# Low halves of plain weight blocks by a ScalarE negative and an accumulating DMA, in a two-layer backbone kernel

## The reference

```python
for l in range(2):
    mc, ml = modulation(c_ctx, w_mod, b_mod), modulation(c, w_mod, b_mod)   # 6 vectors each
    hc, hl = modulate(xc, mc[0], mc[1]), modulate(xl, ml[0], ml[1])
    # layer 0: attention and SSD mixer: u = h @ w_in ... out = [o_a, y] @ w_out
    # layer 1: pooling mixer: u = h @ w_in; pooled @ pool_w (4 groups) * pool_scale; @ w_out
    xc = layer_norm(ALPHA * xc + mc[2] * dc, ln1_g, ln1_b)                   # latent alike
    fc = square(relu(modulate(xc, mc[3], mc[4]) @ w_up)) @ w_down            # 1024 -> 4096 -> 1024
    xc = layer_norm(ALPHA * xc + mc[5] * fc, ln2_g, ln2_b)
```

## Time and profile before

| | us |
|---|---|
| median of 3 runs | 1476.22 (1473.55 to 1477.52) |
| the profiled execution's own time | 1473.62 |
| its span | 1471.8 |
| TensorE, VectorE, ScalarE, GpSimd busy | 1405.8, 1039.6, 542.7, 79.1 |
| mean granted TensorE clock | 0.989 |

### The profile page before, as it was taken

How to read it: one execution, slowest core, us unless ns; L and a number is a source line. 1 busy time by engine, 2 the same in 40 slices (tenths; PEclk the granted TensorE clock), 3 DMA queues, 4 the chain that set the end, 5 groups by cost and what they waited for, 6 DMA issues and landing times.

```text
span 1471.8 us, 22812 instructions
## 1 busy us (share of the span) xinstructions
PE 1405.8 (96%) x8806; PEld 1245.6 (85%) x8806; DVE 1039.6 (71%) x1645; ACT 542.7 (37%) x976; POOL 79.1 (5%) x146
## 2 busy tenths in 40 slices
PE   4999999899999999999999999989999999999996
PEld 3899988666788998998899879868999899889985
DVE  3694566677468976776776796757797677667678
ACT  3333353267435432332233244434443233223322
POOL 1300000011200000000000010001000000000001
PEclk8999999999999999999999999999999999999998
DMA  9701233596713322322221523542332232123141
GB/s 317 220 29 59 87 117 129 167 342 209 249 57 114 130 84 61 115 79 65 85 92 58 208 77 129 186 148 76 121 125 84 62 111 85 59 85 98 59 172 72
DMA packets 132300, 177.47 MB, mean 121 GB/s; under 512 B 4170, under 2 KB 104258, under 8 KB 131698
## 3 DMA queue, kind: packets, MB, share of 16 engines
q1 hardware_dynamic: 123250, 146.46, 31.0%
q0 software_dynamic: 7376, 26.76, 5.3%
q10 hardware_dynamic: 1584, 3.01, 0.5%
HBM read 166.94 MB, written 9.27 MB: 120 GB/s over the span
## 4 chain that ended last, share of the span: by engine, by line
PE 80%; DVE 8%; ACT 5%; DMA 3%; issue 2%; ACTq 0%; POOL 0%; SPq 0%; DVEq 0%
PE ps L779 40%; PE ps L1288 20%; PE ps L761 7%; PE ps L770 4%; PE ps L810 2%; DVE convT L1992 2%; PE ps L1105 2%; ACT h_full L1688 1%; DVE wlo L1896 1%; DMA gate_parts<-modrow 1%; ACT whi L1398 1%; ACT tmp L1688 1%; PE ps L1116 1%; ACT e_att L1608 1%; DMA raw<-in_w_mod_l 1%
## 5 line engine op out<-in xcount | busy, mean ns | idle before, releaser
L1398 ACT ACTIVATE whi<-raw 128x512 fp32r<-128x512 f32 (+2 forms) x186 | 175.4, 953 | 357.1 <-PE ps L779 294.0
L779 PE MATMUL ps<-whi,hid_hi 128*128 128x512 f32 x640 | 249.6, 390 | 0.0
L779 PE MATMUL ps<-wlo,hid_hi 128*128 128x512 f32 x640 | 249.2, 389 | 0.0
L779 PE MATMUL ps<-whi,hid_lo 128*128 128x512 f32 x640 | 249.1, 389 | 0.0
L1896 DVE TENSOR_TENSOR wlo<-raw,whi 128x512 fp32r<-128x512 f32 (+2 forms) x186 | 201.7, 1093 | 24.4 <-ACT whi L1398 21.0
L779 PE MATMUL ps<-whi,h_hi 128*128 128x256 f32 (+1 forms) x480 | 158.7, 331 | 8.7 <-DVE h_lo L2696 5.4
L2325 DVE TENSOR_TENSOR acc<-acc,ps 128x512 f32<-128x512 f32 x120 | 80.3, 684 | 122.0 <-PE ps L779 122.0
L779 PE MATMUL ps<-whi,h_lo 128*128 128x256 f32 (+1 forms) x480 | 153.9, 321 | 0.0
L779 PE MATMUL ps<-wlo,h_hi 128*128 128x256 f32 (+1 forms) x480 | 153.7, 320 | 0.0
L779 PEld LDWEIGHTS ps<-whi,hid_hi 128*128 128x128 f32 x640 | 120.1, 188 | 25.3 <-DVE wlo L1896 0.8
L779 PEld LDWEIGHTS ps<-whi,hid_lo 128*128 128x128 f32 x640 | 120.1, 188 | 25.2
(11 more groups left out here) (337 smaller groups left out, 2669.9 us busy)
## 6 DMA issues: line engine op xcount, KB each, us to landing
raw<-in_w_up_l SPq DMA_DIRECT2D x32, 1024.0 KB, 5.6
raw<-in_w_down_l SPq DMA_DIRECT2D x32, 1024.0 KB, 5.1
raw<-in_w_mod_l SPq DMA_DIRECT2D x28, 1024.0 KB, 5.5
raw<-in_w_in_l SPq DMA_DIRECT2D x12, 1024.0 KB, 5.3
raw_split<-in_w_mod_l SPq DMA_DIRECT2D x8, 1024.0 KB, 6.9
raw<-in_w_out_l SPq DMA_DIRECT2D x5, 1024.0 KB, 6.2
x_spill<-x_tok POOLq DMA_DIRECT2D x10, 512.0 KB, 2.9
x_tok<-x_spill POOLq DMA_DIRECT2D x10, 512.0 KB, 6.0
```

Source lines behind the costliest of these rows:

```text
L779: mm = pe.matmul(out, a_of(still, k), w_of(part, k), start=(first and k == 0 and part == 0 and still == 0), stop=(last and k == nk - 1 and ...
L1398: act.activation(ring_piece(whi, w, g), piece(w, g), ACT.Copy).then_inc(hi_done, 1)
```

## The change

For 26 blocks the low half is made another way. ScalarE, behind each piece of the high half, writes the negative of the raw piece, rounded to fp32r, into `wlo`. Then GpSimd issues a DMA that reads the same 1 MB of weights from HBM again and adds it to `wlo`. TensorE waits for that DMA's semaphore. The blocks are: w_out 1 to 3 of layer 0 and 0 to 3 of layer 1; up 2 and 3 and down 0, 1 and 12 to 15 of both layers; w_in 2 and 3 and the pool block of layer 1. The Strassen blocks, the down blocks between (two of them per turn in the loops and around them), and the two blocks that open each stage behind a norm stay with VectorE. The row stores of layer 1's modulation are issued by GpSimd. Several semaphores are merged. The source of a block's DMA is moved from SP's `load` to `block_source`, unchanged.

```diff
+        NORM_W = tuple(first + n for first in (W_UP[0], W_IN1, W_UP[1]) for n in range(2))
+        def added(w):
+            return w > W_OUT[0] and not strassen(w) and not (S[w_k[w]][0] == "down" and 2 <= S[w_k[w]][2] < 12) and w not in NORM_W
+        def low_ready(eng, w, i=None):
+            if added(w):
+                eng.wait_ge(low_in[w % 2], 16 * ADDED_IN[w])
+            else:
+                eng.wait_ge(lo_done, lin(OPS_LO[w + 1], PER_LO, i))
...
-                    sp.wait_ge(lo_done, lin(OPS[w_ord[j] + 1], PER, i))
+                    if added(w_ord[j]):
+                        sp.wait_ge(neg_done, ADDED[w_ord[j]])
+                    else:
+                        sp.wait_ge(lo_done, lin(OPS_LO[w_ord[j] + 1], PER_LO, i))
...
+            def add_low(w, i=None):                                     # GpSimd
+                pool.wait_ge(neg_done, ADDED[w])
+                src = block_source(w_k[w], i)
+                pool.dma_start(wlo[:, w % 2, :].rearrange("p (k n) -> p k n", n=src.shape[2]), src, accum_op=ALU.add) \
+                    .then_inc(low_in[w % 2], 16)
...
+            def store_rows(m):
+                pool.wait_ge(mod_row, m + 1)
+                for c in range(2):
+                    pool.dma_start(stored_at(m)[:, c], modrow[c:128:32, m % 2, :]).then_inc(tail_st[m % 2], 16)
...
             load_gate_rows(1, 3)
             fetch_x(LAT)
+            for j in range(1, 4):
+                if added(W_OUT[0] + j):
+                    add_low(W_OUT[0] + j)
...
             def mlp(layer):
-                spill_x(layer)
-                fetch_x_again(layer)
+                if added(W_UP[layer] + 2):
+                    add_low(W_UP[layer] + 2)
+                for t in range(LAT):
+                    spill_x(layer, t)
+                for kind, n, i in mlp_steps(pool):
+                    w = w_ord[S.index((kind, layer, n))]
+                    if added(w + 1):
+                        add_low(w + 1, i)
+                    if (kind, n) == ("up", 2):
+                        spill_x(layer, LAT)
+                    if (kind, n) == ("down", 12):
+                        fetch_x_again(layer)
+                if added(w_ord[S.index(("down", layer, 15))]):
+                    add_low(w_ord[S.index(("down", layer, 15))])
...
             norm_share(1)
+            add_low(W_IN1 + 2)
             for g in range(2, 4):
                 pool.wait_ge(pl_f, 2 * (g - 1))
                 pool.dma_start(ic[:, g % 2, :], A["t_icnt"][g].partition_broadcast(P)).then_inc(ic_ld[g % 2], 16)
-            pool.wait_ge(mod_tr, GATE_SUM[1])
-            load_gate_rows(2, 0)
-            pool.wait_ge(gate_rows_ld, 16 * 3)
+                add_low(W_IN1 + g + 1)
+            for m in range(M_TAIL, 48):
+                if m == 46:
+                    pool.wait_ge(mod_tr, GATE_SUM[1])
+                    load_gate_rows(2, 0)
+                    add_low(W_OUT[1])
+                store_rows(m)
+            add_low(W_OUT[1] + 1)
+            pool.wait_ge(sum_rows_ld, 16 * 6)
             load_gate_rows(3, 1)
             spread_gate(2)
+            add_low(W_OUT[1] + 2)
+            add_low(W_OUT[1] + 3)
...
                     act.activation(ring_piece(whi, w, g), piece(w, g), ACT.Copy).then_inc(hi_done, 1)
+                    if added(w):
+                        ins = act.activation(ring_piece(wlo, w, g), piece(w, g), ACT.Copy, scale=-1.0)
+                        if g == len(ring(w)) - 1:
+                            ins.then_inc(neg_done, 1)
...
-                tail_store(KT + f)                                      # ScalarE, in layer 1's pool stage
...
             def split_lo(w, i=None, ops=None):
+                if added(w):
+                    return
```

More of the change, by code:

```diff
@@ L462, in build, with block_source @@
         PER = 4 * len(PIECES) + 4 * 2
+        PER_LO = PER
+        NORM_W = tuple(first + n for first in (W_UP[0], W_IN1, W_UP[1]) for n in range(2))
+        def added(w):
+            return w > W_OUT[0] and not strassen(w) and not (S[w_k[w]][0] == "down" and 2 <= S[w_k[w]][2] < 12) and w not in NORM_W
+        OPS_LO = [0]
+        for w in range(nw):
+            OPS_LO.append(OPS_LO[-1] + (0 if added(w) else len(ring(w))))
+        ADDED = [sum(added(v) for v in range(w + 1)) for w in range(nw)]
+        ADDED_IN = [sum(added(v) and v % 2 == w % 2 for v in range(w + 1)) for w in range(nw)]
+        def low_ready(eng, w, i=None):
[3 more added lines that the diff above has]
+                eng.wait_ge(lo_done, lin(OPS_LO[w + 1], PER_LO, i))
+        def block_source(k, i=None):
+            kind, layer, n = S[k]
+            if kind == "up":
+                c0 = n * BW if i is None else bass.ds(i * (4 * BW) + n * BW, BW)
+                src = A[f"w_up_l{layer}"][:, slice(c0, c0 + BW) if i is None else c0]
+            elif kind == "down":
+                r0 = (n // 2) * CHUNK
+                rows = slice(r0, r0 + CHUNK) if i is None else bass.ds(i * (2 * CHUNK) + r0, CHUNK)
+                src = A[f"w_down_l{layer}"][rows, (n % 2) * 512:(n % 2) * 512 + 512]
+            elif kind == "out":
+                src = A[f"w_out_l{layer}"][(n % 2) * 512:(n % 2) * 512 + 512, (n // 2) * 512:(n // 2) * 512 + 512]
+            elif kind == "pool":
+                src = A["pool_w_l1"].rearrange("g k n -> (g k) n")
+            elif kind == "mod":
+                src = A[f"w_mod_l{layer}"][:, n * BW:(n + 1) * BW]
+            else:
+                src = A[f"w_{kind}_l{layer}"][:, n:n + BW]
+            return src.rearrange("(k p) n -> p k n", p=P)
         def at_ring(buf, its, cols=None):
@@ L690, in norm_share @@
                 for t in range(NT):
+                    if t == 3 and i < 3:
+                        for w in range(2):
+                            first = (W_UP[0], W_IN1, W_UP[1])[i] + w
+                            if added(first):
+                                add_low(first)
                     if i == 3 and t < LAT:
@@ L706, in norm_share, with spill_x @@
                     pool.tensor_tensor(lnrs[:, t, 1:2], lnve[:, t, 0:1], lnrs[:, t, 0:1], ALU.mult).then_inc(ln_rs, 1)
[L708 to L712, removed]
+            def spill_x(layer, t):
+                pool.wait_ge(ln_x, 2 * NT * layer + t + 1)
+                pool.dma_start(A["x_spill"][t * P:(t + 1) * P, :], x[:, t, :]).then_inc(x_re, 16)
             def fetch_x_again(layer):
@@ L1370, in _ @@
             w = W_IN1 + 4
-            pe.wait_ge(lo_done, OPS[w + 1])
+            low_ready(pe, w)
             for f in range(KT):
```

98 lines of the change are left out of this document (42 added, 56 removed).

## The result

| | before | after |
|---|---|---|
| median, us | 1474.88 (1473.52 to 1477.52, 4 runs) | 1609.84 (1606.78 to 1613.77, 4 runs) |
| ratio, 95% interval | 1 | 1.091 [1.088, 1.095] |
| span of the profiled execution | 1471.8 | 1609.3 |
| mean granted TensorE clock | 0.989 | 0.953 |

A forecast was written before the change was run, and what follows sets the result against it. TensorE, busy 96% of the span, was taken as the bound. 1473.6 + 76.8 of pauses + 23.2 of half clock + 2.6 to the median gave 1576 us, range 1520 to 1640; the forecast itself, 1537 to 1615, had chance 0.62.

The forecast's parts named there:

- The sum of the pauses: TensorE's added waits for late low halves at the listed blocks, thirteen terms: 76.8 us.
- T: Time from the end of ScalarE's negative to TensorE's release by the accumulating DMA: taken as 9.1 us.
- The prediction's three parts: Plain 1 MB GpSimd DMA 5.5 us, second read for the add 2.7, collision with SP's next weight load 0.9.
- 13T - 41.5: Thirteen pauses at the listed blocks, each the DMA's delay less that block's slack, added up: 76.8 us.
- the old 5.4 and 1.4: TensorE waits already there before the change: 5.4 us ahead of layer 1's w_out 0, 1.4 (u_pad) at w_in 2.
- The slack formulas: Per block, time from the negative's end to TensorE's first matmul on it; the pause is T less that.
- covered: Blocks with a preceding block's matmuls as cover, such as w_down 13 and 14 or the pool block: no pause.
- The half clock: TensorE at 1.2 instead of 2.4 GHz behind eight new pauses over 5.4 us, 2.9 each: 23.2 us.
- Stores, stream, merged waits: Layer 1's row stores on GpSimd, SP's weight load waiting for the negative, merged semaphores: each taken as 0.
- Relief of VectorE: VectorE's lighter queue: at most 0.8 of the 2.6 us before layer 1's first w_in block, taken as 0.
- The free add: Rival at the accumulating DMAs: they land like a plain transfer, 5.5 us, giving 1512 us; chance 0.17.
- The crawl: Rival at the accumulating DMAs: 13.6 us from negative to release, giving 1645 us; chance 0.17.

The follow-up runs named there:

- Serial: Changed kernel, but SyncE's next weight load into a raw buffer waits for the accumulating DMA instead of the negative: 1570.9 us, ratio 1.066.
- one_block: Kernel before, with only layer 1's last w_down block (15) made by negative and accumulating DMA: 1485.1 us, ratio 1.008.
- experiments 7 and 8: Kernel before with only layer 1's w_down 15 changed, without and with 30 idle matmuls during TensorE's wait: 1485.1 and 1483.2 us.
- experiments 9 and 10: Changed kernel with no block added, only row stores on GpSimd and merged semaphores: 1474.3 us; changed kernel with row stores back on ScalarE: 1612.3 us.
- serial_plain: Changed kernel with SyncE's next load waiting for the transfer, and the transfer copying instead of adding (low halves wrong): 1534.9 us, ratio 1.042.
- plain: Changed kernel with its 26 DMAs as plain copies into wlo instead of accumulating ones (low halves wrong): 1564.5 us, ratio 1.061.
- serial_long: Changed kernel with SyncE's next load waiting for the accumulating transfer, which reads runs of 8 KB (other data): 1563.1 us, ratio 1.061.
- one_block_fill: Kernel before with only layer 1's w_down 15 changed, plus 30 idle matmuls while TensorE waits for it: 1483.2 us, ratio 1.006.

## Why the prediction was right, and where it was off

Forecast: 1576, between 1520 and 1640; measured 1609.8. The mechanism is the one predicted: TensorE waits behind accumulating transfers at the named places and runs at half clock behind them. By its own terms:

- **The sum of the pauses**, 76.8 predicted, 106.7 more idle measured. The mis-sized term is **T**: 9.1 was taken. Read from the traces as for the second w_out block it is 11.2 to 12.8 at w_out, w_up and w_down, 14.2 at layer 1's first w_out block, 14.7 at the pool block and 16.6 at w_in 2; only at the last block of all, with the weight stream over, it is 8.6. The prediction's three parts had two right and one wrong: the plain 5.5 is what a lone plain transfer takes, the add, 2.7, is 3.0, but the collision with SyncE's load, for which 0.9 was left, costs 2.2 to 2.8 at w_down. One more megabyte by the 387 GB/s of the earlier trace rows is 2.7: the sum charged that for the add and not for the neighbour. Runs of 1 KB had nothing beyond their issue and cost about 1 us. Serial, without the load, has T 9.3 and the predicted sum.
- **The sum at the new T.** The thirteen T measured, 12.1 in the mean, put into 13T - 41.5 give 115.5, and the waits at those places are 101 without the old 5.4 and 1.4. The difference is mainly two pauses that an earlier one paid for (below), which no term had. A T of 12.1 is above the 11.5 to which the forecast was said to reach; that the time still fell inside its 1537 to 1615 owes something to those two, and that much is luck.
- The Trainium skill (Collectives: The Full Stack, The bandwidth ceiling) states of the reduce step of a collective that the add is slow by its two source reads. The 3.0 that the add costs alone agrees with that in size, but no run has the second read without the adding, and 0.54 of the 3.0 is issue. The estimate of 2.4 for it by the bytes of the Trainium skill (DMA: Bandwidth & Descriptors, Anatomy of one DMA) is a little under it, and the estimated T of 7.7 is under the 9.3 of one_block.
- **The places.** The rows of four of TensorE's pauses in the kernel after, to be read with the list below:

```profile
985.81 0.90 PE L833 MATMUL ps<-h_hi,whi 128*128 128x320 f32 x2 [13.66 <-DMA wlo<-in_w_in_l]
1022.33 0.90 PE L833 MATMUL ps<-hid_hi,whi 128*128 128x320 f32 x2 [5.77 <-DMA wlo<-in_pool_w_l]
1065.46 0.79 PE L851 MATMUL ps<-whi,h_hi 128*128 128x512 f32 x1 [16.65 <-DMA wlo<-in_w_out_l]
1101.21 0.80 PE L851 MATMUL ps<-whi,h_hi 128*128 128x512 f32 x1 [5.33 <-DMA wlo<-in_w_out_l]
```

| block | predicted | measured |
|---|---|---|
| layer 0 w_out, second and fourth | 8.0, 6.4 | 11.2, 8.8 |
| w_up 2, layer 0 and 1 | 6.7, 6.7 | 8.7, 9.4 |
| w_down 0 and 1, the pair | 0.9, 0.9 | 3.1, 3.2 |
| w_down 12 | 6.0, 6.0 | 8.5, 7.9 |
| w_down 14 | 0, 0 | 3.2, 0 |
| w_down 15 | 7.75, 7.75 | 4.2, 7.2 |
| layer 1 w_in 2 with the old 1.4, pool block | 6.3, 0 | 13.7, 5.8 |
| layer 1 w_out 0, with the old 5.4 | 13.2 | 16.7 |
| layer 1 w_out 2 and 3 | 7.0 | 5.3 |

  Every place with a slack under 9 has its pause, mostly two to three and a half us longer than predicted, as T is. The slack formulas hold with the measured T: at the pool block 14.7 - 9.5 = 5.2 against 5.8, at w_down 14 12.8 - 9.5 = 3.3 against 3.2. Those two were called covered, which is right at T = 9.1 and wrong at 12 or more. Two pauses are shorter than predicted, since an earlier one pays for them: w_down 15 of layer 0 behind the 3.2 of block 14, and w_out 3 of layer 1, whose two groups ahead took 8.47, begun at half clock, and not 5.5. w_in 2 misses by most, 7.4, and its T of 16.6 is 7.5 above 9.1: its transfer has 1 KB runs, stands beside three megabyte loads of SyncE and the constants, and landed in 15.9.
- **The half clock**, 23.2 predicted as eight times 2.9, 30.8 more busy measured. Over stretches of one us, TensorE was busy for 20 us at half clock before and for 81 after; half of the 61 more is 30.5, so the half clock is all of it. The 2.9 was of the right size for one pause (2.4 in experiments 7 and 8). Counting only pauses over 5.4 was not: behind the 3.1 at w_down 0 of layer 0 the 120 matmuls take 29.12 and not 27.23, and behind the 4.2 at w_down 15 of layer 0 the 48 take 12.75 and not 10.9.
- **Stores, stream, merged waits** at 0: shown for the stores and the merged semaphores by experiments 9 and 10; the load's new wait was not tried by itself. **Relief of VectorE** at nothing: of the 8.6 us of old waits 7.8 went where TensorE then waits longer for something else, and 0.8 is relief, as the prediction had it at most. **The loops**: their 120 matmuls take 27.23 and follow each other in 51.86, before and after, as two turns in the chain after show (before, the same starts are 557.28 and 609.14):

```profile
599.59 27.23 PE ps L851 x120
...
651.45 27.23 PE ps L851 x120
```

- **Rivals.** The free add (1512) is what serial_plain nearly is, 1534.9, with the add and the neighbour both gone. The crawl (T = 13.6, 1645) lies as far off as the forecast: T measured is between the two, and the time, 1610, lies midway between 1576 and 1645.

Of the 135 us, by the experiments in a row: 12 for the longer way without a transfer (1474.8 to 1486.4), 48 for a plain transfer, SyncE's load away, in place of VectorE's addition (to 1534.9), 75 for the add and the neighbour together (to 1609.8); taken out alone they are worth 45 and 39, together 84, a little more than both at once. Their parts of half clock are inside.

## What to carry to other kernels

Work that is off the bound engine is worth nothing by its size: 57 us less of VectorE gave back 0.8. Before a step between load and use is put on a DMA, compare its whole latency, in the crowd in which it will run, with the time from its trigger to the first use at each place; with two slots that time is a block's length less the splitting, here 9.4 to 10.7 us. Charge the transfer for the bytes of its neighbour too, when one event starts both. And a lack of pauses at a block in a slowed kernel is no proof of cover: the pause ahead may have made it.

## What the runs showed of the hardware that was not expected

- An accumulating transfer of 1 MB, GpSimd's, with runs of 2 KB, lands in 8.5 to 8.9 us alone, 11.3 beside one 1 MB load. The load beside it hardly suffers: the four w_down loads issued together with a w_down accumulate take 5.6 to 5.8, 5.1 being the median of all 32. The w_up load that meets two accumulates (404.16 us) takes 15.1, and 5.4 in serial.
- GpSimd's issue of an accumulating transfer takes 1.29 us for 512 runs and 1.59 for 1024; of a plain one 0.75 and 0.90 (plain); of an accumulating one with 8 KB runs 0.87 (serial_long). Rows of the kernel after:

```profile
L680 POOL DMA_DIRECT2D wlo<-in_w_down_l x12 | 15.4, 1286 | 723.4 <-ACT wlo L1471 723.4
...
L680 POOL DMA_DIRECT2D wlo<-in_w_up_l x4 | 6.4, 1592 | 39.6 <-ACT wlo L1471 39.2 <-issue 0.3
```

- Other transfers of GpSimd's queue come late behind these: the 0.5 MB spills of x land in 2.9 before and 12.1 after, their reloads in 6.0 and 12.8.
- Thirty matmuls on unused data in a wait of 8 us keep the granted clock at 1.00 behind it (one_block_fill); without them it is 0.50 (one_block).
